# GpSimd's DMA queue in a two-layer encoder trunk: both sends of a pair's outputs ahead of the adding transfer for the weights of the third pair behind it

## The reference

```python
for i in range(DEPTH):                                   # DEPTH = 2
    y = rmsnorm(h, norm_gains[i, 0])
    y = mlstm_mixer(y, ...) if i % 2 == 0 else diff_attention(y, ...)
    h = h + y
    h = h + sq_relu_mlp(rmsnorm(h, norm_gains[i, 1]), mlp_w_up[i], mlp_w_down[i])
h = rmsnorm(h, final_gain)
return h[:, N_META:]

def sq_relu_mlp(y, w_up, w_down):
    u = y @ w_up                                         # 1024 -> 4096
    return jnp.square(jax.nn.relu(u)) @ w_down           # 4096 -> 1024
```

## Time and profile before

| | us |
|---|---|
| median of 3 runs | 1233.13 |
| lowest and highest | 1225.35 and 1234.75 |
| profiled execution, its time | 1227.09 |
| its span in the profile | 1225.4 |
| TensorE busy (matmul) | 1183.9 |
| VectorE busy | 948.7 |
| ScalarE busy | 792.6 |
| GpSimd busy | 176.4 |

### The profile page before, as it was taken

The page is one execution under the profiler, slowest core; times in us unless marked ns, Lnnn a source line. Parts: engine busy times, 40 slices in busy tenths (PEclk is TensorE's granted clock), DMA queues, the critical chain, the costliest instruction groups (busy, mean ns, idle before and its releaser), DMA issues.

```text
span 1225.4 us, 23240 instructions
## 1 busy us (share of the span) xinstructions
PE 1183.9 (97%) x8881; PEld 1138.4 (93%) x8881; DVE 948.7 (77%) x1441; ACT 792.6 (65%) x1401; POOL 176.4 (14%) x215
## 2 busy tenths in 40 slices
PE   9999999999899989989999999999998998998998
PEld 8999999999899989989999999987898998998988
DVE  6889888888868758755678988888986787686754
ACT  6778776656567657555357887876675664765653
POOL 3211210010210210312010000000102112112100
PEclk9999999999999989989999999999998999999999
DMA  7343342444773673684132222222648647657722
GB/s 177 91 120 85 78 105 70 123 124 131 169 157 97 149 164 102 145 191 144 53 88 68 64 62 82 68 69 77 170 130 149 143 124 157 154 109 159 190 86 70
DMA packets 176633, 143.83 MB, mean 117 GB/s; under 512 B 23912, under 2 KB 167328, under 8 KB 176544
## 3 DMA queue, kind: packets, MB, share of 16 engines
q1 hardware_dynamic: 141600, 104.93, 28.7%
q0 software_dynamic: 34816, 37.59, 18.1%
q10 hardware_dynamic: 128, 0.09, 0.0%
HBM read 123.42 MB, written 19.17 MB: 116 GB/s over the span
## 4 chain that ended last, share of the span: by engine, by line
PE 66%; issue 17%; DMA 9%; DVE 5%; ACT 1%; POOL 1%; DVEq 0%; POOLq 0%; ACTq 0%
PE ps L2434 29%; PE ps L2149 18%; PE ps L2384 13%; DMA raw<-in_mlp_w_up_dram 4%; DMA h_sum<-abuf 4%; PE ps L2653 2%; PE ps L2204 1%; DVE lo L1748 1%; PE ps L2222 1%; DVE blocks_f L1788 1%; DVE lof L1735 1%; PE ps L2336 0%; PE ps L2301 0%; DVE lo L1742 0%; DVE blocks_r L1795 0%
## 5 line engine op out<-in xcount | busy, mean ns | idle before, releaser
L2149 PE MATMUL ps<-yh,wh 128*128 128x264 f32 (+1 forms) x704 | 160.6, 302 | 0.0
L810 ACT ACTIVATE hi<-raw 128x1024 fp32r<-128x1024 f32 x128 | 133.4, 1050 | 34.5 <-PE ps L2384 20.0
L2149 PE MATMUL ps<-yl,wh 128*128 128x264 f32 (+1 forms) x704 | 155.4, 295 | 0.0
L2149 PE MATMUL ps<-yh,wl 128*128 128x264 f32 (+1 forms) x704 | 155.3, 295 | 0.0
L1748 DVE TENSOR_TENSOR lo<-raw,hi 128x1024 fp32r<-128x1024 f32 x92 | 112.2, 1220 | 48.6 <-ACT hi L810 47.9
L2434 PE MATMUL ps<-th,hi 128*128 128x264 f32 (+1 forms) x448 | 128.3, 286 | 14.3 <-ACT pu L810 14.3
L2434 PE MATMUL ps<-yl,hi 128*128 128x264 f32 (+1 forms) x408 | 119.9, 294 | 17.6 <-ACT pu L810 17.6
L2434 PE MATMUL ps<-th,lo 128*128 128x264 f32 (+1 forms) x448 | 128.0, 286 | 0.0
L2434 PE MATMUL ps<-tl,hi 128*128 128x264 f32 (+1 forms) x448 | 127.8, 285 | 0.0
L2434 PE MATMUL ps<-yh,hi 128*128 128x264 f32 (+1 forms) x408 | 117.9, 289 | 0.0
L2434 PE MATMUL ps<-yh,lo 128*128 128x264 f32 (+1 forms) x408 | 117.4, 288 | 0.0
(11 more groups left out here) (332 smaller groups left out, 3491.4 us busy)
## 6 DMA issues: line engine op xcount, KB each, us to landing
raw<-in_mlp_w_up_dram SPq DMA_DIRECT2D x32, 1024.0 KB, 8.3
raw<-in_mlp_w_down_dram SPq DMA_DIRECT2D x32, 1024.0 KB, 5.4
raw<-in_diff_w_in_dram SPq DMA_DIRECT2D x24, 512.0 KB, 3.7
raw<-in_mlstm_w_in_dram SPq DMA_DIRECT2D x16, 512.0 KB, 4.6
raw<-in_mlp_w_up_dram POOLq DMA_DIRECT2D x28, 256.0 KB, 4.8
h_sum<-abuf POOLq DMA_DIRECT2D x24, 264.0 KB, 6.8
h_sum<-abuf POOLq DMA_DIRECT2D x24, 256.0 KB, 7.2
raw<-in_mlp_w_down_dram POOLq DMA_DIRECT2D x18, 256.0 KB, 4.7
```

What stands on the lines that cost most here:

```text
L810: return nc.scalar.activation(o, i, ACT.Copy, scale=scale)
L2149: last = mm(ps[:, bank + s, 0:w_], w[:, slot, kb, :], m[:, kb, t0:t0 + w_], start=(kb == 0 and n == 0), stop=(kb == CB - 1 and n == 2))
```

## The change

Inside the same loop, the send of half 1 is no longer put off to the next round, and both sends of pair i stand ahead of the weights of pair i + 3:

```diff
                 for i in range(PAIRS - 7):
-                    if sent_down(i - 1):
-                        send_sum(i - 1, 1)
+                    if sent_down(i):
+                        send_sum(i, 0)
+                        send_sum(i, 1)
                     if i + 3 > PLAIN + 1 and crossed(i + 3):
                         weight_sum(i + 3)
-                    if sent_down(i):
-                        send_sum(i, 0)
```

## The result

The changed kernel takes 1185.24 us (median of 4 runs, 1184.39 to 1185.41), the kernel before 1231.96 us in the same comparison (1225.35 to 1234.75); the ratio is 0.963, 95% interval 0.959 to 0.967. The forecast was 1186. The span of the profiled execution fell from 1225.4 to 1183.6 us, by 41.8; the working of the prediction gave 43.3. One line less stands in the loop, so the lines of code behind it are one lower: L2434 of before is L2433, L810 is L809.

The account below looks back on a forecast made before the run. TensorE's idle time was put mostly to sends landing late, holding ScalarE's copies. Profiled 1227.1 - 31.9 (stalls) - 13.4 (clock) + 2 (adding transfers) = 1183.8 us, placed 2 us up at 1186; range 1179 to 1210.

Parts of the forecast that it names:

- The sends lay behind a wait that they have nothing to do with: GpSimd's queue, pair 5: send issued 4.5 us late behind weights 8; moved to 323.0, it lands in 4 to 6 us.
- All ten stalls go, 31.9 us: TensorE's ten waits for ScalarE's copy out of PSUM (tile pu), 31.9 us in all, vanish once sends land earlier.
- Clock, 13.4 us: TensorE in seven stretches behind stalls: 29.8 us at half clock, of which 13.4 us is lost and would be regained.
- The place, 2 us up: Forecast set 2 us above the sum, at 1186, since other runs shown lie up to 7 us above the profiled execution.
- Adding transfers, 2 us: Adding transfers of weights, now behind both sends of pair i, land later: 2 us cost in all, ends 0 and 18.
- a sign of being wrong: Sign against the forecast: TensorE waits for lo or lof (weights) at S1 or S2 of pairs 8, 16, 24.
- DMA work of 9.2 us in a 10.2 us round fits, narrowly: A round's load, sum and two sends keep DMA engines 9.2 us busy, against 10.2 us of products per pair without stalls.
- Rival A: Stalls go in part: landings stay 8 to 11 us, 21 us of stall remains, 1212 us (late sums alone 1200); chance 0.18.
- Rival B: Gain hidden: something else, VectorE's sums or unready weights, holds P1 at the same time; 1227 to 1233 us; chance 0.05.
- Rival C: Slower: weights of pair i + 3 become bound to TensorE through A22(i); at 12.5 us landings 1244 us; chance 0.04.
- the due time reckoned: First group, weights 8: their sum must land by 335.5 for product S1(8), due to start at 338.7.

Follow-up runs that it names:

- pairs 5 and 6 alone: Against the kernel before: new order for pairs 5 and 6 of each group of down pairs only, old for 4 and 7; 1188.7 us, ratio 0.967.
- The second profile of the changed kernel: The changed kernel, unaltered, run once more beside the last experiment; 1182.2 us, ratio 0.961.
- weights put off to A22: Changed kernel, but adding transfers of pair i + 3 also wait for product A22 of pair i + 1 (i % 8 = 5, 6, 7); 1226.3 us, ratio 0.996.
- that load held back: Changed kernel, but raw-weight loads of pairs 10, 18, 26 wait until the adding transfer of pair 9, 17 or 25 has landed; 1190.1 us, ratio 0.967.
- the second buffer: Order of before, but half 0 of odd pairs goes through a buffer of its own (tile acc); 1213.7 us, ratio 0.987.
- the thin sends: Each send carries 16 columns in place of all; 1179.3 us (0.958) on the changed kernel, 1186.1 us (0.963) in the old order.
- S3: Changed kernel, but adding transfers of pair i + 3 also wait for product S3 of pair i + 1 (i % 8 = 5, 6, 7); 1189.0 us, ratio 0.967.

## Why the prediction was right, step by step

- *The sends lay behind a wait that they have nothing to do with.* Right: pair 5's went at 323.15 (forecast 323.0), and pairs 5 and 6 alone bring almost everything. Forecast for the landing was 4 to 6 us; the two took 4.2 and 6.1, and all sends have a median of 5.9. ScalarE's copy of pair 6 at 328.69 was no longer held by it.
- *All ten stalls go, 31.9 us.* Right to 3.4 us: three short waits remained (0.66, 0.62 and 2.11 us). Idle time fell by 28.4 us, against 29.9 worked out with the 2 us of cost. TensorE's wait for pu is 2.8 us (under 3 forecast); ScalarE's for sends went to nothing (under 15).
- *Clock, 13.4 us.* Right. TensorE's busy time fell by 13.4 us for the same matmuls, and the windows behind the three rests that are left read 1.00. The second profile of the changed kernel has 1168.7 us, 1.8 less, so agreement to the tenth is chance. Of the whole gain a third is clock.
- *The place, 2 us up.* The sum gave 1183.8 for an execution like the profiled one; that one took 1185.4, 1.6 more, nearly all of it the idle time above. The 2 us on top stood for the spread of the kernel before (whose highest run lies 7.7 us above the profiled one, not 7). The changed kernel's four runs lie within 1.0 us, so that step had no object, and that 1186 was met to 1 us is partly luck. The mechanism does not hang on it.
- *Adding transfers, 2 us.* The size was about right (3.4 us of stall), the place wrong in most cases. Weights 16 and 24 took 7.3 to 8.7 us to land, without a stall, as forecast. I took pair 8 (and 16, 24) for the tightest, from VectorE's 4.04 us wait. In the first group of the changed kernel VectorE waited 1.0 us there, and 4.55 us for weights 9. These stand behind pair 6's sends, with the load of pair 10 issued 0.4 us behind them and pair 7's sends after, and landed 9.4 us after the issue. Of TensorE's three rests one is the path that I had reckoned, VectorE's low part at pair 8 in layer 1 (0.62 us), which I had named as a sign of being wrong. The other two come with weights 9 in layer 1 (2.11 us) and weights 25 in layer 0 (0.66 us), for which VectorE waited as well:

```profile
512.48 0.69 DVE L1734 TENSOR_TENSOR lof<-raw 128x512 f32<-128x512 f32 x1 [5.05 <-DMA raw<-in_mlp_w_up_dram]
...
931.31 0.69 DVE L1734 TENSOR_TENSOR lof<-raw 128x512 f32<-128x512 f32 x1 [4.55 <-DMA raw<-in_mlp_w_up_dram]
```

But what held TensorE there was ScalarE. It copies the high part of the summed block (hi<-raw) of pair 9 ahead of pair 8's copy U2 (tile pu), for which product S3(8) waits. In layer 1:

```profile
931.31 1.06 ACT L809 ACTIVATE hi<-raw 128x1024 fp32r<-128x1024 f32 x1 [4.43 <-DMA raw<-in_mlp_w_up_dram]
932.27 0.37 ACT L809 ACTIVATE pu<-ps 128x256 f32<-128x256 f32 x1
...
932.69 0.39 PE L2433 MATMUL ps<-th,hi 128*128 128x256 f32 x1 [2.11 <-ACT pu L809]
```

TensorE was ready at 930.6, so at ScalarE the sum was due by about 929.2, and it landed at 931.3. The prediction counted the due time at VectorE alone. The second profile of the changed kernel has its two stalls (1.06 and 1.63 us) on the same path, and so are 12 of the 15 waits for pu with weights put off to A22.

- *DMA work of 9.2 us in a 10.2 us round fits, narrowly.* Right that it fits, with no more than 3.4 us of stall. But the share came out at 0.94 to 1.08 in such rounds, not the 0.90 worked out, so there was no room left.

  The Trainium skill, "DMA: Bandwidth & Descriptors", section "Queues, rings and completion order", quoted in the prediction, says that a DMA engine takes turns between the queues that have work for it. The longer landings of weights beside loads agree with it (9.4 us with the load of pair 10 beside it, 4.4 us with that load held back), and so does pair 8's load, which landed some 2 us earlier once the sends were gone from beside it.
- *Rival A* left 3.4 us of stall, not 21: sends land in 8.2 us at most. *Rival B* is refuted by the result, and by the second buffer and the thin sends, which cut the wait for pu without the new order. *Rival C*'s mechanism exists: with S3 and with A22 alike weights 8 landed at 335.5, the due time reckoned, and S1(8) stood 0.6 us. But its steps do not add up as it assumed: a delay of 6.5 to 8.6 us for three transfers per group cost 41 us (1226 against 1185), not 70 or more.

## What to carry to other kernels

An in-order DMA queue is a schedule: in front of every issue ask what its wait is for, and put transfers whose data are ready ahead of one that waits for something unrelated. Follow the wait to what it holds at the far end: a buffer is freed by the landing, and the copy into it may stand ahead of the copy that the next product needs. Reckon when a transfer is due at every engine that reads it, not at one: here ScalarE needed the weights sooner than VectorE. Price a stall with the clock behind it, and after the cure look at who shares the DMA engines now.

## What the runs showed of the hardware that was not expected

Short stalls can bring the lower clock. In the kernel with weights put off to A22, TensorE never stood longer than about 2.2 us at once, yet five stretches of 8 us behind its stalls read 0.79. By the prediction's reckoning that is 5 x 16 x 0.21 = 16.8 us at the lower level and 7.6 us lost, an estimate. Its busy time was 12.5 us more than in the changed kernel (1183.0 us), so clock is the larger part and not all; why matmuls stood further apart at 1.00 too is not shown (64 in the 8 us of the second row, 67 in the last). Windows of that kernel behind stalls of 1.97 and 2.23 us, then two of the kernel before, both behind stalls of 1.81 us:

```profile
1040.80:1048.80 8.00, 8.00 (x55) 8.00 (x56) 5.63 (x8) 4.93 (x8) 0.27 (x1) 0.79 0.61 158
1130.60:1138.60 8.00, 7.87 (x64) 7.69 (x65) 5.57 (x8) 4.83 (x8) 1.44 (x2) 1.00 0.53 149
...
1042.84:1050.84 8.00, 8.00 (x55) 8.00 (x56) 2.98 (x4) 4.47 (x7) 3.07 (x3) 0.79 0.56 108
1117.36:1125.36 8.00, 8.00 (x67) 8.00 (x68) 4.43 (x6) 4.48 (x7) 3.07 (x3) 1.00 0.58 139
```

Stalls of one length had either outcome, and with the second buffer even one of 3.17 us kept 1.00; no run here settles what decides it. The second surprise is the thin send of 8.4 us above: 16 columns of 128 rows, as late as a whole one.
